# Head norms worked beside the next weight stream, and the memory's parts made without the memory's norm

## What is computed

```python
# rwkv7_mixer, the end: a norm per head of 64, gain, bias, bonus, gate
mean = jnp.mean(y, axis=-1, keepdims=True)
var = jnp.mean(jnp.square(y - mean), axis=-1, keepdims=True)
y = ((y - mean) * lax.rsqrt(var + RW_GN_EPS)).reshape(bsz, seqlen, RW_W) * cast(ln_w) + cast(ln_b)
out = (y + bonus) * g                      # g = sigmoid(gd) @ g2, the second low-rank product
# diff_attention, the end: an rms norm per head of 128
return rmsnorm_2(o, subln_g) * (1.0 - lam_init)
# then, after each of the three mixers
h = h + y @ w_mix_out
h = h + attention(rmsnorm(h, xattn_norm), rmsnorm(mem, mem_norm), wq, wkv, wo)
```

## Time and profile before

| | |
|---|---|
| median of 3 executions | 3589.91 us (3586.78 to 3590.45) |
| profiled execution | 3583.65 us, its span 3581.9 us |
| mean granted TensorE clock | 0.97 of full |
| TensorE matmuls busy | 94% of the span |
| VectorE, ScalarE busy | 54%, 33% |

### The profile page before, as it was taken

How to read it: one execution, slowest core, us unless ns; L and a number is a source line. 1 busy time by engine, 2 the same in 40 slices (tenths; PEclk the granted TensorE clock), 3 DMA queues, 4 the chain that set the end, 5 groups by cost and what they waited for, 6 DMA issues and landing times. The chain is left out here.

```text
span 3581.9 us, 49550 instructions
## 1 busy us (share of the span) xinstructions
PE 3363.2 (94%) x21374; PEld 2761.6 (77%) x21374; DVE 1916.6 (54%) x2703; ACT 1194.9 (33%) x1702; POOL 5.5 (0%) x6
## 2 busy tenths in 40 slices
PE   7999996779999999999996789999999998999998
PEld 5888885668788888888875768788887757878886
DVE  4434646755454445444747654443456766457475
ACT  3223433124332233223423134332233274334243
POOL 0000000000000000000000000000000000000000
PEclk9999997899999999999997889999999999999999
DMA  3323222014123232323220013122223202323232
GB/s 124 108 84 112 83 88 65 3 49 136 59 94 101 93 101 94 100 94 102 93 84 4 3 63 132 65 94 100 94 100 117 83 1 88 118 71 100 94 99 72
DMA packets 78201, 301.73 MB, mean 84 GB/s; under 512 B 8946, under 2 KB 9586, under 8 KB 77344
## 3 DMA queue, kind: packets, MB, share of 16 engines
q1 hardware_dynamic: 77984, 298.56, 24.8%
HBM read 296.40 MB, written 6.06 MB: 84 GB/s over the span
## 5 line engine op out<-in xcount | busy, mean ns | idle before, releaser
L315 DVE TENSOR_TENSOR w_lo<-ring,w_hi 128x1024 fp32r<-128x1024 f32 (+1 forms) x508 | 652.9, 1286 | 534.6 <-ACT w_hi L308 534.5
L329 PE MATMUL ps<-xa_hi,w_hi 128*128 128x512 f32 x1728 | 682.7, 395 | 32.0 <-DVE w_lo L315 29.3
L330 PE MATMUL ps<-xa_lo,w_hi 128*128 128x512 f32 x1728 | 675.7, 391 | 0.0
L331 PE MATMUL ps<-xa_hi,w_lo 128*128 128x512 f32 x1728 | 675.6, 391 | 0.0
L308 ACT ACTIVATE w_hi<-ring 128x1024 fp32r<-128x1024 f32 (+1 forms) x508 | 554.3, 1099 | 297.7 <-DMA ring<-in_ffn_in_dram 73.7
L329 PE MATMUL ps<-xb_hi,w_hi 128*128 128x512 f32 x1248 | 489.4, 392 | 0.0
L331 PE MATMUL ps<-xb_hi,w_lo 128*128 128x512 f32 x1248 | 485.8, 389 | 0.0
L330 PE MATMUL ps<-xb_lo,w_hi 128*128 128x512 f32 x1248 | 485.6, 389 | 0.0
L329 PEld LDWEIGHTS ps<-xa_hi,w_hi 128*128 128x128 f32 x1728 | 326.0, 189 | 111.3 <-DVE w_lo L315 30.1
L330 PEld LDWEIGHTS ps<-xa_lo,w_hi 128*128 128x128 f32 x1728 | 326.5, 189 | 68.5 <-issue 1.9
L331 PEld LDWEIGHTS ps<-xa_hi,w_lo 128*128 128x128 f32 x1728 | 326.2, 189 | 68.7
(11 more groups left out here) (353 smaller groups left out, 3484.8 us busy)
## 6 DMA issues: line engine op xcount, KB each, us to landing
ring<-in_ffn_in_dram SPq DMA_DIRECT2D x176, 512.0 KB, 3.4
ring<-in_ffn_out_dram SPq DMA_DIRECT2D x64, 704.0 KB, 4.0
ring<-in_mix_in_dram SPq DMA_DIRECT2D x58, 512.0 KB, 3.4
ring<-in_up_dram SPq DMA_DIRECT2D x44, 512.0 KB, 3.4
ring<-in_w_in_dram SPq DMA_DIRECT2D x22, 512.0 KB, 3.5
ring<-in_down_dram SPq DMA_DIRECT2D x16, 704.0 KB, 4.1
ring<-in_mix_out_dram SPq DMA_DIRECT2D x16, 512.0 KB, 3.5
ring<-in_xk_dram SPq DMA_DIRECT2D x16, 512.0 KB, 3.4
```

Of the source, the lines that this page charges most:

```text
L315: dve.tensor_tensor(core.w_lo[j][:, 0:width], core.ring[j][:, 0:width], core.w_hi[j][:, 0:width].bitcast(F32), ALU.subtract).then_inc(self ...
L329: pe.matmul(out, hi, x_hi, start=(k == 0), stop=False)
L330: pe.matmul(out, hi, x_lo, start=False, stop=False)
L331: last = pe.matmul(out, lo, x_hi, start=False, stop=(k == k_tiles - 1))
```

## The change

The norm stages after the mixers are removed. Their work goes into the long stage, into two new classes with the same methods: `GroupNorm` after rwkv and `HeadNorm` after the attention mixer. `Mixed` now knows which y tiles exist already (`EARLY`, five of eight, or four) and which the norm still has to finish (`LATE`). TensorE multiplies the early tiles of weight blocks 0 to 3 into four banks, with the norm's sums behind block 0 and its spread behind block 1, then the late tiles of blocks 0 to 3, then blocks 4 to 7 whole. `out` takes eight banks.

The memory's parts are made from the memory times its gain alone. Its root goes onto what comes of them: `keys` are multiplied by it on VectorE when they leave the bank (before: a copy on ScalarE), `values` on ScalarE by a column. So a reciprocal of 256 columns becomes one of 258 and moves behind block 7, the eight scalings (L1210) go, and upper and lower parts take the gain. In rwkv's first stage the second low-rank product is moved behind both spreads.

```diff
@@ Mixed
+    def tensor_all(self, pe, out, aside):
+        late.tensor_first(pe)
+        for i in range(self.BEGUN):
+            st.some(pe, out.first + i, late.EARLY, out.x, to(i), None if i else ready, closes=False)
+            if i == 0:
+                late.tensor_sums(pe)
+            if i == 1:
+                late.tensor_spread(pe)
+        for i in range(self.BEGUN):
+            st.some(pe, out.first + i, late.LATE, out.x, to(i), None if i else ready,
+                    opens=False).then_inc(st.used, 1)
+        for i in range(self.BEGUN, out.n):
+            st.multiply(pe, out.first + i, KD, out.x, to(i))
+            aside(pe, i)
+    def scalar_all(self, act, memory):
+        self.upper(act, late.EARLY[0])
+        st.split_hi(act, 0)
+        for k in late.EARLY[1:]:
+            self.upper(act, k)
+        st.split_hi(act, 1)
+        late.scalar_squares(act)
+        st.split_hi(act, 2)
+        late.scalar_root(act)
+        st.split_hi(act, 3)
+        for n, k in enumerate(late.LATE):
+            act.wait_ge(self.phase["y_normed"], n + 1)
+            self.upper(act, k)
+        memory.scalar_squares(act)
+        for k in range(KD):
+            memory.scalar_upper(act, k)
+    def vector_all(self, dve, memory):
+        self.lower(dve, late.EARLY[0])
+        st.split_lo(dve, 0)
+        for n, k in enumerate(late.EARLY[1:]):
+            self.lower(dve, k)
+            late.vector_first(dve, n)
+        for n in (1, 2):
+            st.split_lo(dve, n)
+        late.vector_invert(dve)
+        st.split_lo(dve, 3)
+        late.vector_last(dve)
+        for k in late.LATE:
+            self.lower(dve, k)
@@ GroupNorm.vector_last
+        for m in range(3):
+            dve.wait_ge(ph["y_spread"], m + 1)
+            dve.scalar_tensor_tensor(y[:, m], y[:, m], core.v1("ln_w", m), core.ps[:, m, :], ALU.mult, ALU.mult)
+        for m in range(3):
+            dve.scalar_tensor_tensor(y[:, m], y[:, m], core.v1("ln_b", m), self.bonus[:, m], ALU.add, ALU.add)
+        for m in range(3):
+            dve.tensor_tensor(core.y[:, 5 + m, :], y[:, m], self.g[:, m], ALU.mult).then_inc(ph["y_normed"], 1)
@@ MemoryBlock.vector_all
         for i in range(KD):
             self.out.vector(dve, i)
-            st.split_lo(dve, self.out.first + i + LEAD)
+            if i:
+                st.split_lo(dve, self.out.first + i + LEAD)
             if i == 2:
-                self.memory.vector_root(dve)
-            if i == 4:
-                self.memory.vector_lower(dve)
+                self.memory.vector_joins(dve)
+            for k in {3: (0, 1), 4: (2, 3, 4), 5: (5, 6, 7)}.get(i, ()):
+                self.memory.vector_lower(dve, k)
+        self.memory.vector_root(dve)
@@ Project
-            dve.tensor_tensor(self.dst(i), self.core.ps[:, self.bank(i), :], self.core.root[:, :],
+        dve.tensor_tensor(self.dst(i), self.core.ps[:, self.bank(i), 0:self.n_tok], self.root,
@@ rwkv, first stage, TensorE
-            for m in range(3):
-                pe.matmul(ps[:, 3 + m, :], lora_g[:, m * P:(m + 1) * P], big[:, RG, :], ...)
             pe.wait_ge(squared, 1)
             for m in range(3):
                 last = sums_by_token(pe, core, 6, m, three(norm)[:, m])
@@
+            for m in range(3):
+                if m == 2:
+                    pe.wait_ge(opened, 4)
+                pe.matmul(ps[:, 6 + m % 2, :], lora_g[:, m * P:(m + 1) * P], big[:, RG, :], ...)
```

More of the change, by code:

```diff
@@ L318, in multiply, with some @@
     def multiply(self, pe, n, k_tiles, x, out, ready=None, aside=None):
+        self.some(pe, n, range(k_tiles), x, out, ready, aside).then_inc(self.used, 1)
+    def some(self, pe, n, tiles, x, out, ready=None, aside=None, opens=True, closes=True):
         core, j = self.core, n % RING
         pe.wait_ge(self.parted, n + 1)
-        for k in range(k_tiles):
+        for k in tiles:
             if aside is not None:
@@ L328, in multiply @@
             hi, lo = core.w_hi[j][:, k * P:(k + 1) * P], core.w_lo[j][:, k * P:(k + 1) * P]
-            pe.matmul(out, hi, x_hi, start=(k == 0), stop=False)
+            pe.matmul(out, hi, x_hi, start=(opens and k == tiles[0]), stop=False)
             pe.matmul(out, hi, x_lo, start=False, stop=False)
-            last = pe.matmul(out, lo, x_hi, start=False, stop=(k == k_tiles - 1))
-        last.then_inc(self.used, 1)
+            last = pe.matmul(out, lo, x_hi, start=False, stop=(closes and k == tiles[-1]))
+        return last
 def tiles_of(parts):
@@ L1193, in tensor_sum @@
     def tensor_sum(self, pe):
-        ph = self.phase
+        ph, ps = self.phase, self.core.ps
         pe.wait_ge(ph["mem_joined"], 3)
-        pe.matmul(self.core.ps[:, 7, 0:MEM], self.core.c("ones"), self.squares[:, 0:MEM], start=True,
-                  stop=True).then_inc(ph["mem_summed"], 1)
+        pe.wait_ge(ph["added"], 1)
+        pe.matmul(ps[:, 4, 0:MEM], self.core.c("ones"), self.squares[:, 0:MEM], start=True, stop=True)
+        for t in range(2):
+            last = pe.matmul(ps[:, 4, MEM + t:MEM + t + 1], self.squares[:, t * P:(t + 1) * P], self.core.c("ones")[:, 0:1],
+                             start=True, stop=True)
@@ new lines, in vector_root, with scalar_upper, vector_lower @@
+        dve.reciprocal(self.roots, self.roots).then_inc(self.phase["mem_known"], 1)
+    def scalar_upper(self, act, k):
+        act.activation(self.parts[0][:, k, :], self.mem[:, k, :], ACT.Copy,
+                       scale=self.gain(k)).then_inc(self.phase["mem_upper"], 1)
+    def vector_lower(self, dve, k):
+        dve.wait_ge(self.phase["mem_upper"], k + 1)
+        dve.scalar_tensor_tensor(self.parts[1][:, k, :], self.mem[:, k, :], self.gain(k),
+                                 self.parts[0][:, k, :].bitcast(F32), ALU.mult, ALU.subtract).then_inc(self.phase["mem_lower"], 1)
@@ L1479, with __init__ @@
 class MemoryBlock:
-    def __init__(self, phase, w_mixed, dram, w_q, w_k, w_v, w_o, layer, norm, gain_m, then):
+    def __init__(self, phase, w_mixed, dram, w_q, w_k, w_v, w_o, layer, norm, gain_m, then, late):
         core, big = phase.core, phase.core.big
@@ L1509, in tensor_all @@
     def tensor_all(self, pe):
-        self.out.tensor_all(pe, lambda pe, i: self.memory.tensor_sum(pe) if i == 1 else None)
+        self.mixed.tensor_all(pe, self.out, lambda pe, i: self.memory.tensor_sum(pe) if i == 5 else None)
         self.keys.tensor_all(pe)
@@ L1950, in _ @@
             last.then_inc(spread, 1)
+            for m in range(3):
+                if m == 2:
+                    pe.wait_ge(opened, 4)
+                pe.matmul(ps[:, 6 + m % 2, :], lora_g[:, m * P:(m + 1) * P], big[:, RG, :], start=True,
+                          stop=True).then_inc(low_rank, 1)
             pe.wait_ge(rated, 1)
@@ L1976, in _ @@
             act.activation(e_in, cum_w, ACT.Exp).then_inc(grown, 1)
+            for m in range(3):
+                act.wait_ge(low_rank, m + 4)
+                act.activation(three(g)[:, m], ps[:, 6 + m % 2, :], ACT.Copy).then_inc(opened, 1)
     v_n, k_n, b_n, a_n = (s[n].rearrange("p (q f) -> p q f", q=4) for n in range(4))
```

302 lines of the change are left out of this document (147 added, 155 removed).

## The result

The changed kernel takes 3565.2 us, the median of five runs (3558.75 to 3570.49). The kernel before, run on the same chip, takes 3588.0 (3584.38 to 3590.45). The medians differ by 22.8 us, where 26.7 were predicted. The ratio of the two, estimated from all runs, is 0.993 with a 95% interval of 0.9918 to 0.9941, which is 21 to 29 us less. The profiled execution took 3558.75 us with a span of 3556.9, 25.0 us shorter than the span before (3581.9).

A forecast was written before the change was run, and what follows sets the result against it. TensorE (busy 94%) was taken to lose time where norm and long stages follow each other, with VectorE's loop as pace behind output 0. Three long stages 22.3 + rwkv 4.4 = 26.7 us off 3589.9 gives 3563 us, range 3552 to 3577.

The forecast's parts named there:

- The loop and its contents: Long stage, output 0 to 7: VectorE's loop with ScalarE sets the pace, 4.75 us a step, 36.2 us with inserted work.
- output 7 to the first value matmul: Long stage's end: 4.9 us to key block 2, 17.4 for six key blocks, 0.4 for the moved reciprocal and key product.
- TensorE's wait: Long stage: TensorE waits again at key blocks 1 and 2 for weight blocks' lower parts, 2 to 5 us together.
- with nothing idle between: Kernel before, second layer: outputs 6 and 7 taken 4.75 us apart on VectorE, read as without idle time.
- The way to output 0: Long stage from the norm's first instruction to output 0: TensorE's list, 27.1 us in layer 2, 25.1 after the attention mixer.
- T to the sums: From the norm's first instruction (T): averages 5.46 us in layer 2, 2.81 in layer 1, then block 0's early tiles, 3.4.
- sums to the spread: TensorE's list after rwkv: the norm's sums, 2.80 us, then early tiles of block 1, 3.4 us.
- spread to output 0: After rwkv: spread 2.84 us, early tiles of blocks 2 and 3 6.8, late tiles of block 0 2.0, result 0.4.
- rival A: Long stages: clock falls behind sums and spreads, 1.9 us each, and rwkv gains 2.8; gain 13.7, 3576.2 us; chance 0.13.
- rwkv: rwkv's first stage, twice: second sums no longer wait for the low-rank product; 2.2 us each, 4.4 together.
- Rival B: Long stages: the loop isn't the pace, only TensorE's list counts; another 7.3 us a stage, gain 49, 3541 us; chance 0.09.
- Rivals C and D: C: loop 1.0 us a step longer, gain 8.7, chance 0.04. D: half clock through cut-up blocks, 3599 to 3621 us, 0.04.

The follow-up runs named there:

- experiment 5: Changed kernel with ScalarE's weight split ahead of each output's square and upper part, and all but one of each norm's sums removed; 3532.3 us, ratio 0.9851.
- experiments 4 and 8: Changed kernel with ScalarE's weight split put ahead of each output's square and upper part, run twice; 3543.7 us (ratio 0.9876), then 3544.5 us (0.9874).
- experiment 3: Kernel before with only rwkv's first stage in the new order; 3579.7 us, ratio 0.9975.
- Experiments 6 and 9: Changed kernel with ScalarE's weight split first and the norm sums cut into twos to fours between tiles, run twice; 3543.3 us (0.9873), then 3543.1 us (0.9875).
- experiments 1: Kernel before with only the norms moved into the stream, the memory's parts and rwkv's first stage as before; 3581.0 us, ratio 0.998.

## Why the prediction was right, step by step

**The time.** 3563 was predicted, 3565.2 measured; the sum was 26.7 us, the spans of the two profiled executions differ by 25.0 and the medians by 22.8.

**The loop and its contents: right.** Output 0 to output 7 was worked out at 36.2 us and took 35.75; the plain step at 4.75 and took 4.74; three halvings at 2.41 and took 2.40; output 7 to the first value matmul at 22.7 and took 22.8 to 23.1. TensorE's wait came back at key block 1, 2.88 us in the second layer, as foretold. One reading was wrong and did no harm to the number: the step of 4.75 us was called one "with nothing idle between", where VectorE waits 1.66 us for ScalarE. Output 0 to the first value matmul, predicted at 58.9 to 59.6, took 58.5, 58.9 and 59.2.

**The way to output 0: mis-sized.** This is the term that failed, "Sum 27.1 us to output 0" (24.5 in layer 1, 25.1 in the second block). Measured: 27.6 (28.5 in layer 1, 27.2 in the second block). So the forecast had the three ways to output 0 together 7.0 us shorter than before, and they came out 0.4 shorter, while the part behind output 0 gave 16.2 us where 15.4 were forecast. By pieces, measured less predicted, for layer 1, layer 2 and the second block:

| | layer 1 | layer 2 | second block |
|---|---|---|---|
| T to the sums | 8.75 - 6.2 = +2.5 | 7.86 - 8.86 = -1.0 | 7.2 - 7.6 = -0.4 |
| sums to the spread | 7.8 - 6.2 = +1.6 | 7.8 - 6.2 = +1.6 | 8.0 - 5.6 = +2.4 |
| spread to output 0 | -0.1 | -0.1 | +0.1 |

The middle line is the fall behind the sums, 1.6 us each by experiment 5, and in the second block 0.8 more for the sums themselves (3.76 for 2.9; 24 records in 2.80 us, as in the earlier trace rows, would have given 3.7 for its 32). The fall was priced in rival A, with 1.9, and not in the forecast, though the row at 2093 us showed one behind these very sums in layer 2. In layer 1 of the same trace there is none, and its spread ran at full clock, so the rows of before spoke for either. The first line has two causes. One is the state in which the averages run: their six records took 2.81 and 5.46 us before, 5.46 and 4.08 after. It differs between executions of one kernel too: experiments 4 and 8 are the same kernel, with 4.44 and 5.46 us in one execution and 4.48 and 4.37 in the other. The Trainium skill (TensorE: Matmul & The Clock Gate, Part 1) says that the same kernel can meet the change of clock at different points from run to run; these numbers agree. The other is a wait that the sum didn't have: the prediction let layer 1's tiles follow the averages at once, 6.2 us in all, where VectorE's lower parts allow no less than the 7.9 of experiment 5.

**rwkv: right.** 2.2 us each was taken from a range of 1.4 to 3.9; 2.3 each was measured here, and 1.9 and 3.9 in experiment 3.

**What made up for the miss.** The stages gave 16.5 + 4.6 = 21.1 us against 26.7, but the span 25.0. Of the 3.9 us between, 2.3 lie behind the third long stage, which the change doesn't touch, and 1.7 of these are the clock. The kernel before has a stretch at half clock some 92 us behind that stage, and eight records there took 5.40 us; the changed kernel has no such stretch, and the same eight took 3.70. The window and the records of before:

```profile
3148.00:3151.00 3.00, 3.00 (x4) 1.10 (x4) 0.00 (x0) 0.00 (x0) 0.00 (x0) 0.50 0.00 0
...
3147.62 5.40 PE L1279 MATMUL ps<-big 128*128 128x512 f32 x8 [0.69 <-ACT big L1376]
```

The records of the changed kernel:

```profile
3124.98 3.70 PE L1279 MATMUL ps<-big 128*128 128x512 f32 x8 [0.69 <-ACT big L1376]
```

Experiments 6 and 9 are one kernel, and the trace of 9 has such a stretch at that place where that of 6 has none: this is luck and no work of the change. The rest isn't pinned down. So the total was met more closely than its terms deserve.

**Rival A** was half right: one fall in each stage, behind the sums, and none behind the spreads. **Rival B's** price was right (7.3 us a stage; experiment 4 gave 6.9, 7.3 and 5.6 behind output 0, and its 3543.7 us stand near B's 3541), and so was the reason for not believing it of this kernel. What the text missed is that the reason, a wait of VectorE on ScalarE in the loop, is itself an order that one swap undoes. **Rivals C and D** did not come: the step stayed at 4.74 us, and in both layers the clock was full from the spread on for ten microseconds of the cut-up blocks.

## What to carry to other kernels

Where two engines hand work back and forth in a loop, look at what each does first. The partner's wait of 1.66 us a step was worth some 20 us of this kernel (ratios 0.993 and 0.9876), nearly as much as the whole rearrangement, for one swapped line. On the kernel before the same line gave 11 us, since TensorE's own list lay only 3.6 us below the loop there: ask not only what sets the pace but what would set it next. Moving work off an idle stretch into a full stream gains only what the next pace-setter lets through, so sum up that loop step by step, as was done here, and then ask what in it could go. Put a price on what moved work does to its new neighbours: here a clock fall that costs 1.6 us or more behind each unbroken set of narrow matmuls.

## What the runs showed of the hardware

- Behind 12 float32 matmuls of two columns in one piece at full clock (24 records, 2.73 us), TensorE's granted clock fell to 0.50 for about 3 us in both layers of the changed kernel, and in its second block behind 16 of one column (32 records, 3.76 us), while matmuls of 512 columns were running. All twelve long stages of the changed kernel and experiments 1, 4 and 8 have the fall, three of them for twice as long. Behind 24 matmuls of 128 columns by 64 rows (48 records, 2.84 us), the spread, it stayed at 1.00 in both layers. With one sum left (experiment 5), and with the sums in twos to fours met at full clock (experiments 6 and 9, five stages), no fall began behind them.
- The same interleaved stream of wide and narrow matmuls met at half clock stayed there for 20 us in one execution, and rose within some 3 us, before the narrow ones began, in another.
- In layer 2 of the changed kernel the clock stood at 0.50 for the 6.5 us behind TensorE's wait of 2.88 us, and output 7 to the first value matmul took 23.1 us. In layer 1 the clock stayed full behind the same wait, TensorE waited another 1.9 us for lower parts of weight blocks (1.64 and 0.24), and it took 22.8. Where VectorE sets the pace, those 6.5 us at half clock cost 0.3 us.
